# The down projections of the second block's feed-forward part as seven block products, with sums and low parts made by adding transfers

## The reference

```python
u = rms_norm(h, norm_mlp_pre[l])
hid = jnp.square(jax.nn.relu(jnp.einsum("btd,df->btf", u, w_up[l])))   # 1024 -> 4096
m = jnp.einsum("btf,fd->btd", hid, w_down[l])                          # 4096 -> 1024
h = h + rms_norm(m, norm_mlp_post[l])
```

## Time and profile before

| | us |
|---|---|
| median of 3 runs | 1020.32 |
| lowest, highest | 1019.99, 1020.34 |
| span of the profiled execution (first to last instruction) | 1018.8 |
| PE busy | 1010.3 |
| DVE, ACT, POOL busy | 758.5, 556.8, 232.6 |
| the loop of up and down tiles and its tail | 842.7 to 1018.8 |

### The profile page before, as it was taken

One profiled execution on the slowest core, in us unless ns is written; L12 is line 12 of the kernel. 1 busy time (PEld: TensorE's weight loads), 2 busy tenths in 40 slices (PEclk: granted clock), 3 DMA queues, 4 the chain that ended last, 5 costly groups with the idle time before them and its releaser, 6 DMA issues.

```text
span 1018.8 us, 14751 instructions
## 1 busy us (share of the span) xinstructions
PE 1010.3 (99%) x5688; PEld 851.1 (84%) x5688; DVE 758.5 (74%) x1208; ACT 556.8 (55%) x848; POOL 232.6 (23%) x322
## 2 busy tenths in 40 slices
PE   9999999999999999999999999999999999999997
PEld 6877788888888877788888888998888888888886
DVE  6997568788777887578787778888865457766665
ACT  6575566545556466656554556845544455334433
POOL 0572600000000272800000004019947620000000
PEclk9999999999999999999999999999999999999999
DMA  9641545555554351365554544553445556564541
GB/s 362 232 159 59 176 155 207 190 182 207 194 180 173 114 218 42 125 221 193 212 195 177 207 168 163 171 201 119 170 150 184 204 186 227 191 214 174 182 149 41
DMA packets 27894, 180.24 MB, mean 177 GB/s; under 512 B 3120, under 2 KB 3248, under 8 KB 7472
## 3 DMA queue, kind: packets, MB, share of 16 engines
q1 hardware_dynamic: 27824, 179.30, 49.5%
HBM read 178.24 MB, written 1.05 MB: 176 GB/s over the span
## 4 chain that ended last, share of the span: by engine, by line
PE 97%; DVE 1%; ACT 1%; DMA 0%; issue 0%; SPq 0%; DVEq 0%
PE pb L747 17%; PE pb L752 10%; PE pb L609 9%; PE pb L610 9%; PE pb L612 8%; PE pb L772 6%; PE pb L771 6%; PE pb L773 6%; PE pb L754 3%; PE pb L1017 2%; PE pb L970 2%; PE pb L673 1%; PE pb L672 1%; PE pb L674 1%; PE pb L709 1%; PE pb L985 1%
## 5 line engine op out<-in xcount | busy, mean ns | idle before, releaser
L1895 DVE TENSOR_TENSOR wlo<-raw,whi 128x2048 fp32r<-128x2048 f32 (+1 forms) x125 | 282.8, 2265 | 102.4 <-ACT whi L1374 102.2
L1374 ACT ACTIVATE whi<-raw 128x2048 fp32r<-128x2048 f32 x159 | 298.5, 1881 | 60.5 <-PE pb L612 34.6
L2772 POOL TENSOR_TENSOR wlo<-raw,whi 128x256 fp32r<-128x256 f32 x268 | 206.8, 810 | 318.9 <-ACT whi L1374 315.2
L747 PE MATMUL pb<-hb,whi 128*128 128x512 f32 x770 | 183.7, 389 | 0.0
L747 PEld LDWEIGHTS pb<-hb,whi 128*128 128x128 f32 x770 | 144.6, 188 | 30.4
L609 PE MATMUL pb<-whi,hb 128*128 128x512 f32 x336 | 134.2, 399 | 0.1
L610 PE MATMUL pb<-wlo,hb 128*128 128x512 f32 x336 | 130.9, 390 | 0.0
L612 PE MATMUL pb<-whi,hb 128*128 128x512 f32 x320 | 124.9, 390 | 0.0
L752 PEld LDWEIGHTS pb<-hb,wlo 128*128 128x128 f32 x880 | 112.8, 191 | 4.3
L752 PE MATMUL pb<-hb,wlo 128*128 128x256 f32 x880 | 114.2, 283 | 0.0
L772 PE MATMUL pb<-wlo,gh 128*128 128x512 f32 x280 | 109.2, 390 | 0.0
(11 more groups left out here) (404 smaller groups left out, 1558.8 us busy)
## 6 DMA issues: line engine op xcount, KB each, us to landing
raw<-wst SPq DMA_DIRECT2D x159, 1024.0 KB, 4.8
raw<-wst SPq DMA_DIRECT2D x10, 512.0 KB, 4.3
gb<-gains SPq DMA_DIRECT2D x3, 512.0 KB, 6.4
XN<-xt SPq DMA_DIRECT2D x2, 512.0 KB, 5.3
X<-x SPq DMA_DIRECT2D x1, 1024.0 KB, 12.1
out<-X SPq DMA_DIRECT2D x4, 256.0 KB, 2.0
PQ<-prm SPq DMA_DIRECT2D x1, 909.0 KB, 4.5
raw<-wst SPq DMA_DIRECT2D x2, 256.0 KB, 7.3
```

Source lines behind the costliest of these rows:

```text
L747: e.matmul(b[:, :], wh[:, k, s], hb2[:, k, :, :].rearrange("p i q -> p (i q)"), start=k == 0, stop=False)
L1374: e.activation(whi[:, split_slot(m), 0:w], raw[:, m % RAW, 0:w], ACT.Copy).then_inc(*hi(m))
L1895: e.tensor_tensor(wlo[:, split_slot(m), s], raw[:, m % RAW, s], whi[:, split_slot(m), s].bitcast(F32), ALU.subtract).then_inc(*lo_v(m))
L2772: g = e.tensor_tensor(wlo[:, split_slot(m), s], raw[:, m % RAW, s], whi[:, split_slot(m), s].bitcast(F32), ALU.subtract)
```

## The change

Only the feed-forward part of the second block changes.

**Down tiles.** A down tile is a product of 2 x 2 blocks of hidden values (two token halves, two feature halves) with 2 x 2 blocks of weights (two feature halves, two column halves). It is now computed with seven block products (`quarter_products`; a form of Strassen's method, due to Winograd) in place of eight, each again of three matmuls of 512 columns, 21 in all. Each product is summed over all 16 tiles in its own bank, 1 to 7, and the four outputs are put together from the seven sums once at the end. Three products (4, 6, 7) use weights that are sums of blocks, and four (3, 5, 6, 7) use hidden values that are sums. The weights are laid out in four quarters of 512 columns. For each tile:
- POOL issues a transfer that adds quarter 0 (from HBM) to quarter 2 in `raw` (`weight_blocks`, semaphore `s_t1`), and one that adds quarter 2 to a copy of quarter 3 that SP has loaded into `sums_at` (semaphore `s_q3`).
- DVE makes two more sums (`weight_sums`), the low part of the sums (`sums_low`, 1536 columns), of the tile itself (`split`), of the hidden values and of their sums (`features_low`), and the hidden sums themselves (`token_blocks`).
- ACT makes the high parts (`quarters_high`, `sums_high`, `features_high`).

**Up tiles.** Seven banks belong to the products, so an up tile is done in two blocks of 512 columns (`wide_block`), both in bank 0 from tile 2 on, each evicted by ACT (`evict`). From up tile 2 on the low part is not made by DVE: ACT writes the negated high part into `wlo` and POOL issues a transfer that adds `raw` to it (semaphore `s_low`).

**Order.** PE's round is: block 0 of up tile j, products 4, 6, 7 of down tile j-2, block 1 of up tile j, products 1, 2, 3, 5 of down tile j-1.

The diff, cut to its core (the removed loops called `wide`, `down` and `down_quarter` on PE and `summed` and two splits on DVE; the combination of the seven products at the end is left out):

```diff
...
+        PRODUCTB = {1: 5, 2: 6, 4: 7, 3: 4, 5: 1, 6: 2, 7: 3}
...
         def lows(m):
 
+            if m in by_dma:
+                return (low_landed(m),)
             return (lo_g[m], lo_v[m]) if low_shared(m) else (lo_of(m)[m],)
...
+        ups = [tile_at[2, "up", j, 0] for j in range(16)]
+        downs = [tile_at[2, "down", j, 0] for j in range(16)]
+        last_out = tile_at[2, "out", 1, 1]
+        ODD_SLOT = 3
+        by_dma = ups[2:]
...
+        def up_bank(j, i):
+
+            return (0, 1)[i] if j == 0 else (2, 0)[i] if j == 1 else 0
...
+            def wide_block(m, i, bank, ready):
+
+                wh, wl = (w.rearrange("p (k c) -> p k c", k=8) for w in parts(m))
+                s, b = slice(128 * i, 128 * i + 128), PB[bank]
+                q.wait_ge(*hi[m])
+                bank_free(bank)
+                for k in range(7):
+                    q.wait_ge(*ready[k])
+                    e.matmul(b[:, :], wh[:, k, s], hb2[:, k, :, :].rearrange("p i q -> p (i q)"), start=k == 0, stop=False)
+                q.wait_ge(*ready[7])
+                for low in lows(m):
+                    q.wait_ge(*low)
+                for k in range(8):
+                    e.matmul(b[:, 0:L], wl[:, k, s], hh[:, k, :], start=False, stop=False)
+                mm = e.matmul(b[:, :], wh[:, 7, s], hb2[:, 7, :, :].rearrange("p i q -> p (i q)"), start=False, stop=True)
+                mm.then_inc(*(used(m) if i else half_used(m)))
+
+            def quarter_products(j, *names):
+                m = downs[j]
+                wh, wl = (w.rearrange("p (k c) -> p k c", k=4) for w in parts(m))
...
+                pair = {1: (ah[:, 0, 0, :], al[:, 0, 0, :], wh[:, 0, :], wl[:, 0, :]),
+                        2: (ah[:, 0, 1, :], al[:, 0, 1, :], wh[:, 1, :], wl[:, 1, :]),
...
+                        7: (th_[:, 0, :], tl_[:, 0, :], sh[:, 2, :], sl[:, 2, :])}
+                for n in names:
+                    if n in (1, 2, 3, 5):
+                        weights_ready(m)
+                    else:
+                        q.wait_ge(*sums_lo[j])
+                    if n in (1, 2, 4):
+                        q.wait_ge(*gl_done[m])
+                    else:
+                        q.wait_ge(*tokens_lo[j])
+                    b = PRODUCTB[n]
+                    if j == 0:
+                        bank_free(b)
+                    o, (high, low, w_high, w_low) = PB[b][:, :], pair[n]
+                    e.matmul(o, high, w_high, start=j == 0, stop=False)
+                    e.matmul(o, high, w_low, start=False, stop=False)
+                    mm = e.matmul(o, low, w_high, start=False, stop=j == 15)
+                    if j == 15:
+                        mm.then_inc(*product(n))
+                    elif n == 5:
+                        mm.then_inc(*used(m))
+                    elif n == 7:
+                        mm.then_inc(*sums_used(j))
...
+                wide_by_k(ups[0], (0, 1), lp, [hh_done[("lp", 2), "column", k] for k in range(8)])
...
+                for j in range(1, 16):
+                    wide_block(ups[j], 0, up_bank(j, 0), lp)
+                    free[up_bank(j, 0)] = ff_low[2, j, 0]
+                    if j > 1:
+                        quarter_products(j - 2, 4, 6, 7)
+                    wide_block(ups[j], 1, up_bank(j, 1), lp)
+                    free[up_bank(j, 1)] = ff_low[2, j, 1]
+                    quarter_products(j - 1, 1, 2, 3, 5)
+                quarter_products(14, 4, 6, 7)
+                quarter_products(15, 1, 2, 3, 6, 7, 4, 5)
...
-                    e.activation(whi[:, split_slot(m), 0:w], raw[:, m % RAW, 0:w], ACT.Copy).then_inc(*hi(m))
+                    e.activation(parts(m)[0][:, 0:w], raw[:, m % RAW, 0:w], ACT.Copy).then_inc(*hi(m))
+                    if m in by_dma:
+                        e.activation(parts(m)[1], raw[:, m % RAW, :], ACT.Copy, scale=-1.0).then_inc(*minus_hi(m))
...
+
+                def evict(j, i):
+                    q.wait_ge(*(used if i or not j else half_used)[ups[j]])
+                    if j > 1:
+                        q.wait_ge(*ff_sum[2, j - 2])
+                    elif j:
+                        q.wait_ge(*squares[("lp", 2), 1, 1])
+                    e.activation(E[:, 2 * (j % 2) + i, :], PB[up_bank(j, i)][:, :], ACT.Copy).then_inc(*ff_low(2, j, i))
+
+                def quarters_high(j):
+                    q.wait_ge(*landed(downs[j]))
+                    q.wait_ge(*landing(s_t1, j))
+                    q.wait_ge(*used[slot_before(downs[j])])
+                    e.activation(parts(downs[j])[0], raw[:, downs[j] % RAW, :], ACT.Copy).then_inc(*hi(downs[j]))
+
+                def sums_high(j):
+                    q.wait_ge(*summed_w[j])
+                    q.wait_ge(*landing(s_q3, j))
+                    q.wait_ge(*(used[downs[13]] if j == 15 else sums_used[j - 1] if j else used[last_out]))
+                    e.activation(sums_parts(j)[0], sums_at[j % 2], ACT.Copy).then_inc(*sums_hi(j))
+
+                def features_high(j):
                     q.wait_ge(*ff_glu[2, j])
                     if j >= 2:
-                        q.wait_ge(*used[tile_at[2, "down", j - 2, 0]])
-                    e.activation(gh[:, j % 2, :, :], z, ACT.Copy).then_inc(*gh_done(tile_at[2, "down", j, 0]))
+                        q.wait_ge(*sums_used[j - 2])
+                    e.activation(gh[:, j % 2, :, :], (cc, th)[j % 2][:, :, :], ACT.Copy).then_inc(*gh_done(downs[j]))
+                    q.wait_ge(*tokens_sum[j])
+                    e.activation(tokens_high[j % 2], token_sums, ACT.Copy).then_inc(*tokens_hi(j))
+                square_half(n, 0)
+                square_half(n, 1)
+                quarters_high(0)
+                for j in range(16):
+                    evict(j, 0)
                     if j:
-                        ahead(2, "down", j - 1, 0)
+                        features_high(j - 1)
+                    if j == 15:
+                        quarters_high(15)
+                    if j:
+                        sums_high(j - 1)
+                    evict(j, 1)
+                    if 0 < j < 15:
+                        quarters_high(j)
+                    if j < 14:
+                        split(ups[j + 2])
+                features_high(15)
+                sums_high(15)
...
+                def weight_sums(j):
+                    r, o = raw[:, downs[j] % RAW, :], sums_at[j % 2]
+                    q.wait_ge(*landed(downs[j]))
+                    q.wait_ge(*landing(s_t1, j))
+                    if j > 1:
+                        q.wait_ge(*sums_lo[j - 2])
+                    e.tensor_tensor(o[:, 512:1024], r[:, 1536:2048], r[:, 1024:1536], ALU.add).then_inc(*dve())
+                    q.wait_ge(*q.prev)
+                    e.tensor_tensor(o[:, 0:512], o[:, 512:1024], r[:, 512:1024], ALU.add).then_inc(*summed_w(j))
+
+                def sums_low(j):
+                    q.wait_ge(*sums_hi[j])
+                    high, low = sums_parts(j)
+                    e.tensor_tensor(low, sums_at[j % 2], high.bitcast(F32), ALU.subtract).then_inc(*sums_lo(j))
+
+                def token_blocks(j):
+                    z = (cc, th)[j % 2][:, :, :]
+                    for i in range(2):
+                        q.wait_ge(*ff_low[2, j, i])
+                    b = 2 * (j % 2)
+                    both = E[:, b:b + 2, :].rearrange("p f (h q) -> p f h q", h=2)
+                    e.tensor_tensor(z, both[:, :, 0, :], both[:, :, 1, :], ALU.add).then_inc(*ff_sum(2, j))
+                    q.wait_ge(*ff_sum[2, j])
+                    e.scalar_tensor_tensor(z, z, 0.0, z, ALU.max, ALU.mult).then_inc(*ff_glu(2, j))
+                    q.wait_ge(*ff_glu[2, j])
+                    if j:
+                        q.wait_ge(*tokens_lo[j - 1])
...
+                    e.tensor_tensor(ts[:, 0:2, :], g[:, 0:2, :], g[:, 1:4:2, :], ALU.subtract).then_inc(*dve())
+                    q.wait_ge(*q.prev)
+                    e.tensor_tensor(ts[:, 2, :], ts[:, 0, :], g[:, 3, :], ALU.add).then_inc(*dve())
+                    q.wait_ge(*q.prev)
+                    e.tensor_tensor(ts[:, 3, :], ts[:, 2, :], g[:, 2, :], ALU.subtract).then_inc(*tokens_sum(j))
+
+                def features_low(j):
+                    m = downs[j]
+                    q.wait_ge(*gh_done[m])
+                    e.tensor_tensor(gl[:, j % 2, :, :], (cc, th)[j % 2][:, :, :], gh[:, j % 2, :, :].bitcast(F32),
+                                    ALU.subtract).then_inc(*gl_done(m))
+                    q.wait_ge(*tokens_hi[j])
+                    e.tensor_tensor(tokens_low[j % 2], token_sums, tokens_high[j % 2].bitcast(F32),
+                                    ALU.subtract).then_inc(*tokens_lo(j))
+                weight_sums(0)
+                split(downs[0])
                 for j in range(16):
                     if j == 1:
+                        input_scale()
+                    if 0 < j < 15:
+                        split(ups[j + 1])
```

(38 more changed lines are left out.)

178 lines of the change are left out of this document (120 added, 58 removed).

## The result

The changed kernel takes 1140.43 us (median of 4 runs, 1138.89 to 1140.91) where the kernel before takes 1020.21 (1019.99 to 1020.34): ratio 1.1175, 95% interval 1.116 to 1.1191. Slower was forecast, but the forecast of 1090 and its range up to 1125 fell short: the change costs 120 us, not 70.

What follows compares the result with a forecast made beforehand. PE bounds the kernel before; the change adds a wait on POOL's adding transfers. Span 1018.8 plus start 10.4, rounds 49.6, last tile 2.2, end 2.9 and clock 5 (+70.1) gives 1088.9, forecast 1090 us, range 1052 to 1125.

Steps and rivals of the forecast that it cites:

- T(j): Landing of POOL's first adding transfer for down tile j, the one that makes the weight sum in raw.
- the forecast's own signs of being wrong: T(j) within 1 us of the negated copy, PE's wait ending on something else, or x outside 5 to 10.
- x: Time from the end of ACT's negated copy to T(j); taken as 8 us, bounds 5.6 and 10.2.
- its two rows: Trace rows used to price x: a 1 MB load landing after 4.8 us, a 256 KB store after 2.0.
- the DMA engines become the bound: Rival: 3.75 MB a round take 11.6 us, 16.2 if adding counts double; 1100 to 1125, chance 0.20 with full clock loss.
- the first ring: Dependency over ACT's copies, x, DVE's sums and low parts, and PE: two rounds take 21.1 + x, 14.55 us each.
- ACT's own: Second ring: T(j), down copy, two up copies, x, T(j+1); 5.6 + x = 13.6 us a round.
- the third ring: Load of down tile j, small transfer, weight sums, split, which releases the next load: 10.7 to 12.0 us.
- the small transfer is not held by the large one: Rival: the small transfer lands early and the ring over the load decides; 1051, or 1050 to 1065, chance 0.18.
- S(1): Start of PE's products (1, 2, 3, 5) following up tile 1's second block; forecast 858.7, +10.4 us against before.
- Clock: PE's idle time lets some products start at half clock: 0 to 19 us in all, taken as +5.
- The fastest rival: Nothing waits: products save 10.9 us, end costs 2.9, last tile about 1; 1013, needs x below 0.9, chance 0.03.

Runs made afterwards that it cites:

- a: Changed kernel with only POOL's order changed: the 256 KB adding transfer into raw is issued ahead of the 1 MB one; 1076.31 us.
- e: Changed kernel with the edits of a and b together; 1073.0 us.
- b: Changed kernel with only DVE's order changed: low part of down tile j-1 made before the weight sums of tile j; 1157.89 us.
- n: c with the plain 1 MB copy issued by ACT on its own queue, behind its negated copy; 1107.16 us.
- d: Changed kernel with the up tiles' low parts made by DVE, no negated copy on ACT and no 1 MB transfer; 1069.58 us.
- l: Changed kernel without its three adding transfers a round, those parts of the computation left out, all orders kept; 1019.63 us.
- c: Changed kernel with the 1 MB transfer copying raw instead of adding it (up tiles' low parts then wrong); 1117.33 us.
- i: Changed kernel with the 1 MB adding transfer and negated copy halved to columns 1024 to 2047, DVE making the rest; 1116.21 us.
- h: Changed kernel with two weight sums computed by POOL, no small adding transfers, the 1 MB one kept, and b's order on DVE; 1054.49 us.
- k: e with the halved (512 KB) adding transfer of i; 1051.4 us.
- m: Changed kernel with the 1 MB adding transfer reading the weights from HBM in place of raw; 1143.49 us.
- g: Changed kernel without adding transfers: POOL computes two weight sums and the up tiles' low parts, with b's order on DVE; 1084.71 us.
- j: h with the halved (512 KB) adding transfer of i; 1040.78 us.

## Why the prediction was wrong

By its own steps, against the profiled span of 1139.2 (forecast 1088.9, a miss of 50.3):

- **Place and waits: right.** DVE waits for T(j) at the weight sums, PE behind it at product 1, ACT at the down tile's copy; POOL issues the 1 MB transfer right behind ACT's negated copy. Two of the forecast's own signs of being wrong came as well: x is outside 5 to 10, and a round is longer than 15.9 us.
- **x: the step that failed.** "It is nearer to neither row, so I take 8" should have been 12.7, beyond even its bound of 10.2. (The line through its two rows was also misread: 4.8 and 2.0 us give 3.73 us a MB and not 3.65, which moves its x by 0.1 to 0.2 us only.) Two things were missing in it. POOL does not issue the small transfer behind the large one at once: its issue takes 0.9 us and then it waits 2.1 us for the down tile's load. The forecast had nothing for that wait. And the price was built from transfers that have the DMA engines nearly to themselves, the two on POOL's queue, with only a rounding up for the loads beside them. In fact SP's 256 KB copy and a 1 MB load behind it, let go within 1.2 us of the 1 MB adding transfer (957.84, 958.26 and 957.13), are issued ahead of the small transfer, which took 9.4 us for it. The DMA engines' work is 14.6 us a round, and most of it, 12.3 us at full share, lies inside x.
- **The rival "the DMA engines become the bound": right in size, wrong in form.** It had 11.6 to 16.2 us a round; measured are 14.6. I compared that with my round of 14.55 as if the larger of the two would win. But a burst is in series with what releases it: some 6 us around ACT's copies in which the DMA engines have little to do (2.2 us at a share of 0.46 and 3.8 at 0.21). The burst, 12.3 us, and those are the round of 18.2. Kernels a and e show the case that I had priced, with the burst spread out: 14.5 us a round.
- **Which ring decides: wrong.** The forecast gave the first ring up to x = 10 and ACT's own (5.6 + x) beyond. At 12.7 that formula gives 18.3, close to the measured 18.2, but only because x holds the wait for the load. It is the third ring, over the load, that decides: load 4.8, 0.3 to wake, small transfer 9.4, weight sums and low part 3.7. The forecast knew this ring and put it at 10.7 to 12.0, with 2.0 to 3.3 for the small transfer. Cutting it alone does not pay (b), since the loads then go into the burst and ACT's ring becomes the longer one.
- **The third rival, "the small transfer is not held by the large one":** n shows that even on separate queues it is held, by what was issued ahead of it. It lands early only where no 1 MB copy or adding transfer is ahead (4.9 us in a, 5.2 in d), and even that is well over the 2.0 to 3.3 given; a round of d is 13.8 us, 1.8 over the 12.0.
- **Rounds:** 14 of 18.40 in place of 14.55, from 860.63 to 1118.16: +53.9 us. This is more than the whole miss.
- **Start:** S(1) at 860.63, forecast 858.7: +1.9. ACT's last copy ended at 848.0 as forecast (848.3), and x was 10.4 here, not 8; what follows it took 2.2 us for 2.4.
- **Last tile and end:** 21.0 us from product 1 of tile 15 to the end of the span, forecast 13.3 + 8.2 = 21.5: -0.5. The last matmul ends at 1130.35, 12.2 us after product 1 and not 13.3, and the tail takes 8.9, not 8.2.
- **Clock:** the granted clock is 0.50 in the windows from 955.0 and 957.2, and after PE's stall the twelve matmuls of the four products start 0.43 us apart (861.62, 862.05, 862.48) in place of 0.23, as foreseen. But +5 was wrong for this kernel: PE is not in the ring that decides, and ACT waits at the down tile's copy for the transfer and no longer for PE in all 14 rounds, so it costs nothing. The margin is thin, 0.15 us in one round and 0.35 at 969.58: with a shorter x it would have counted.
- **The fastest rival, 1013 if x were hidden:** l puts it at 1019.63. It gave away 1 us at the last tile and 2.9 at the end; measured are 4.6 together, another 2.7 at the start, and the saving is 7.6 (0.54 in 14 rounds), not 10.9. The 0.68 us a round was right where nothing waits (0.66 in 13 of the rounds of l).

By the fit of the Trainium skill ("DMA: Bandwidth & Descriptors", the anatomy of one DMA on the GpSimd path) the estimate was x = 5.0 and 1061 us; measured are 12.7 and 1140. The measurement decides: the fit does not hold for an adding transfer in a burst, 1 MB took 8.7 us, not 4.4. Nor does it for the plain 1 MB copy in c (8.0 us). The row on which the forecast had tested it, 4.8 us, was a load issued by SP and not by POOL.

What stays open is the size of three runs: i, h and k ended 6, 9 and 13 us above the ranges of the theories that they went with. They fit the picture (the landing of a transfer depends on what was issued ahead of it), but no run prices the loads' share in it. The engines' work per transfer is worked out from mean shares of several kernels and is good to some tenths of a us.

## What to carry to other kernels

Draw the transfers of a round on a time line before pricing any of them: what one event releases shares the 16 engines, whichever queue issued it. Look at every wait of the engine that issues, too: 2.1 us of x were POOL waiting for a load. If the ring is "burst, then compute that releases the next burst", its length is the sum of the two, and a mean DMA share of 0.8 is no sign of room. Issue the transfer that something waits for ahead of the large ones (64 us here for one line moved, 9 of them at the start and 55 in the rounds), and be wary of cutting a ring by letting loads go earlier, which can fill the same burst (17 us lost in b). Before saving an eighth of some matmuls in a loop of 16 rounds, price its first round, its start and its end: here they took back all of it (l).

## What the runs showed of the hardware that I had not expected

- An adding transfer costs the DMA engines about 1.6 times a plain one of its size: 4.7 against 2.9 us for 1 MB (changed kernel, c and d), and reading from HBM in place of SBUF does not make it land sooner (m: 9.2 against 8.7 us).
- The two 256 KB adding transfers cost 2.8 us a round together (d 9.8, l 7.0 from its row, 2.36 MB x 0.68 / 229), about 5.7 us a MB: no cheaper for being small.
- POOL and DVE operations on SBUF hold each other up, and which one pays differs by place: in g a 256-column piece on POOL takes 2.9 us beside a 2048-column subtraction of DVE that keeps its 2.28; in j DVE's 256-column subtraction takes 849 ns for 425 beside a piece of POOL.
- A 256 KB adding transfer landed after 4.2 to 4.9 us with the DMA engines at a share above 1 (a) and after 9.4 us at the same share (changed kernel): what was issued ahead of it counts, not how busy the engines are.
- ACT and DVE with 8.9 us of work each in a round of 10.35 did not hold PE up (l, by its row, rounds after the first). Tight budgets were not the problem; the transfers were.
